# Two blocks and a mixture of experts on one core: the split operands of the mixers and of the third part at other byte offsets

## The chip, the core and the metric

The kernel runs on 1 core of one Trainium2 chip. The metric is the time of one execution in device microseconds, the median of the runs; lower is better. A profiled execution gives the trace from which the rows below are taken. Its span, from the first to the last instruction, is shorter than the execution's time, since start and end lie outside it.

## The reference

Two layers of a hybrid block, then a third block with a mixture of experts, all float32, on a sequence of 256 tokens with D = 1024:

```python
for i in range(2):
    x = x + 0.5 * swiglu(rms_norm(x, ffn1_norm[i]), ffn1_w_gate[i], ffn1_w_up[i], ffn1_w_down[i])
    h = rms_norm(x, mix_norm[i])
    proj = h @ w_in[i]
    z, xbc, dt_raw, q, k, v = jnp.split(proj, splits, axis=-1)
    y_ssd = ssd_mixer(silu(conv(xbc)), dt_raw, z, ...)
    y_att = dilated_attention(rms_norm(q), rms_norm(k), v)
    x = x + concatenate([y_ssd, y_att]) @ w_out[i]
    x = x + 0.5 * swiglu(rms_norm(x, ffn2_norm[i]), ...)
# third part: one more layer
u = modulate(rmsnorm(h, g_norm1), sh1, sc1)
proj = u @ w_in_2                       # conv branch, q, k, v, r, gates
h = h + ga1 * (gate0 * y_conv + gate1 * y_gla) @ w_out_2
u2 = modulate(rmsnorm(h, g_norm2), sh2, sc2)
h = h + ga2 * hierarchical_moe(u2, ...) # 32 experts
out = modulate(rmsnorm(h, g_final), shf, scf)
```

## The kernel before

Nearly every large product is split for accuracy: an operand A is held as a high part Ah, rounded to the float32r format, and a low part Al = A - Ah, and the product is three matmuls into one PSUM bank, high times low, low times high, high times high. The helper `three` (L776 to L782) issues them. Its arguments are `wh, wl` (the stationary operand, loaded into the array before each matmul) and `mh, ml` (the moving operand, streamed past it). In the rows of the profile a matmul reads `out<-moving,stationary`; so `misc<-xh,ring_low` streams xh past weights of ring_low, and `misc<-ring_low,xh` the other way round. The lines L780, L781 and L782 are those three matmuls, in that order.

The stages, in order of time:

- FFN 0, mixer 0, FFN 1, FFN 2, mixer 1, FFN 3 (two layers), then the third part with its own input projection, and the experts from about 1530 us on.
- An FFN (`ffn`, `gate_up`, `down`) streams the normalised rows xh, xl past the columns of the gate and up weights: high parts in `high_b`, low parts in `ring_low`. Each `gate_up` is 48 matmuls of 128x256. Then `down` streams weights (`high_r`, `ring_d_low`) past the hidden rows `hidh`, `hidl`, 12 matmuls of 128x512.
- A mixer first has 8 blocks of columns for the convolution; two of them unsplit, six split (`X_SPLIT`, in `ssd_and_projections`): xh, xl are the moving operand there, weights the stationary one. Then come 16 blocks through `project`, 48 matmuls each, in which the roles are swapped: weights (high parts in `ring_d_low` or `ue`, low parts in `ring_low`) move past xh, xl, 128 tokens at a time. Between the blocks stand short transposes and state products of the state-space scan. The out-projection later keeps its own split rows in the same space as xh, xl.
- The third part's input projection uses u2h (which lies on the space named `ue`) and u2l. `cols_split` has them as the moving operand, 21 blocks; `toks_split` has them as the stationary one, 4 blocks; 48 matmuls of 128x256 each. Between them stand the pair products (L1236) of the gated linear attention, whose data VectorE prepares.
- In the experts `ue` holds the gathered tokens as the stationary operand, weights move past in 512 columns.

SP's queue loads 1 MB blocks into a ring of 4 slots; a slot is freed by the last matmul that reads it. ACT rounds the high part, VectorE subtracts (`ring_low<-ring,...`). All of this is a fixed order written by hand; each engine runs its own stream and waits on semaphores.

**Where the operands lie.** All these buffers stand in one region of SBUF that begins with the ring. Bytes from the ring's start, modulo 512, follow from the sizes in the code. The rings take 12288 words, a multiple of 512 bytes. All parts have multiples of 128 words, except `xraw`, which has NX * (CONV_K - 1) = 48 words more (192 bytes). So whatever lies behind xraw is at 192, the rest at 0:

| operand | place before | place after |
|---|---|---|
| ring_low, ring_d_low, high_b, high_r, in_pc, in_rT | 0 | 0 |
| `ue` as weights of the mixers and tokens of the experts | 0 | 0 |
| xh, xl in the FFNs and in the out-projection | 192 | 192 |
| hidh, hidl | 192 | 192 |
| xh, xl in both mixers | 192 | 320 |
| u2h, u2l in the third part | 0 | 192 |

High and low halves of one operand lie a multiple of 512 bytes apart, and so do the slices of 128 or 256 words that one matmul takes.

Of the kernel before, what the change touches and what calls it, by code (L numbers as in the profile page):

```python
# [14 lines left out]
P = 128  # L15
SEQ = 256
# [24 lines left out]

# [93 lines left out]
def two_blocks(nc, d, out):  # L135
# [33 lines left out]
    with ctx:  # L169
# [11 lines left out]
        A_V2, A_PC, A_RT, A_OSQ = 6144, 8192, 10240, 26368  # L181
        rings = SLOTS * SLOT + SLOTS * SLOT_D
        A_Z = 2 * 2 * SEQ + NT * D + NX * (SEQ + CONV_K - 1) + NX * SEQ
# [23 lines left out]
        A_HIGH = 2 * 2 * SEQ + NT * D  # L207
# [3 lines left out]
        ue = over("ue", [KD, 2, 2 * CAP])  # L211
# [47 lines left out]
        xsc = part([NT, D])  # L259
        yatt = xsc  # L260
# [21 lines left out]
        yT = part([2 * KD, SEQ])  # L282
        btok = part([GROUPS, P])
# [20 lines left out]
        at[0] = 2 * 2 * SEQ + NT * D  # L304
# [22 lines left out]
        osq = part([KD, SEQ])  # L327
        zpad = part([NC2, SEQ + CONV_W - 1])
# [7 lines left out]
        u2h = ue[:, :, :, :].rearrange("p a b c -> p a (b c)")  # L336
# [16 lines left out]
        at[0] = here + 4 * GH * SEQ + 2 * GH * P + GH * P + KD * SEQ  # L353
# [3 lines left out]
        at[0] = A_X + 2 * KD * SEQ  # L357
# [24 lines left out]
        he = [a[:, :, :].rearrange("p a b -> p (a b)").rearrange("p (a b) -> p a b", a=CPE)  # L382
# [236 lines left out]
        def high_w(b):  # L619

            if b % HIGH_W < 2:
                return ring_d_low[:, 2 * (b % HIGH_W):2 * (b % HIGH_W) + 2, :].rearrange("p a b -> p (a b)")
            return ue[:, :, :, :].rearrange("p a b c -> p (a b c)")
# [153 lines left out]
        def _(pe):  # L777
# [57 lines left out]
            def first_gate_up(m0, n0, u):  # L835

                b = claim_bank(m0)
# [31 lines left out]
            def gate_up(m0, n0, i, c):  # L869
# [12 lines left out]
            def down(m0, n0, d0, g0, i, c, start, stop, between=()):  # L882
# [23 lines left out]
            def ffn(f, a, u, pieces=()):  # L906
# [5 lines left out]
                gate_up(m0, n0, 0, 1)  # L912
                pe.wait_ge(row_ready, u + 1)
                down(m0, n0, d0, NF * f, 0, 0, True, False)

                with pe.Fori(0, (NF - 2) // 4) as i:
                    for j in range(4):
                        gate_up(m0, n0, i, j + 2)
                        down(m0, n0, d0, NF * f, i, j + 1, False, False)
                for p in pieces[:1]:  # L920
                    modulation(p)
                down(m0, n0, d0, NF * f, 0, NF - 1, False, True, pieces[1:])
# [55 lines left out]
            def project(l, m, b):  # L978

                n = RING["win", l] + 8 + b  # L980
# [9 lines left out]
            def ssd_and_projections(l, a):  # L990
                n0 = RING["win", l]
                for j in range(8 - X_SPLIT):
# [698 lines left out]
        def _(act):  # L1691
# [29 lines left out]
            def rows_high(u, gain):  # L1721

                for q in range(4):
# [1589 lines left out]
```

## Time and profile before

| | |
|---|---|
| median of 3 runs | 2104.0 us |
| lowest, highest | 2101.42, 2104.66 us |
| span of the profiled execution | 2093.1 us |
| PE (matmul) busy | 2053.3 us, 98% |
| VectorE busy | 1644.7 us, 79% |
| ACT busy | 1212.5 us, 58% |
| DMA queues together | 61% of 16 engines' span, 230 GB/s |
| granted TensorE clock, mean | 0.997 |

The profiled execution's own time was not recorded apart from its span; the median of the runs is 10.9 us over the span. The page's busy time of PE counts the whole life of a matmul (some 276 ns for 256 columns), and these lives overlap, since the next matmul starts before the last has ended. What a matmul costs is the distance from its start to the start of the next, called its slot below. It is read from the view in order of time.

### The profile page before, as it was taken

The page shows a single profiled execution, that of the slowest core. Times are in us where ns is not written, and L with a number is a line of the kernel's source. Part 1 is how long each engine was busy: PE and PEld are TensorE (multiplying, and loading weights), DVE is VectorE, ACT ScalarE, POOL GpSimd, SP SyncE. Part 2 cuts the span into 40 slices and gives each one's busy share as a digit, 9 for nine tenths or more (in the row PEclk, how much of TensorE's full clock was granted, in tenths as well). Part 3 has the DMA queues.
Part 4 walks back from the last instruction along what each step waited for, and adds up shares of the span by engine and source line. Part 5 has one row for each costly group of instructions (what it writes and reads, how often), then busy time and mean ns, then how long its engine had stood idle before and what let it go on. Part 6 is the DMA issues. An engine that isn't in the chain of part 4 may idle for free. (4 is left out here: it accounts for less than half of the span.)

```text
span 2093.1 us, 35595 instructions
## 1 busy us (share of the span) xinstructions
PE 2053.3 (98%) x13737; PEld 1840.0 (88%) x13737; DVE 1644.7 (79%) x2070; ACT 1212.5 (58%) x1527; POOL 454.9 (22%) x237
## 2 busy tenths in 40 slices
PE   9999999999999999999999999999999999999997
PEld 8998999789999999999789998999877877777775
DVE  5776868557767875768557766998699999999998
ACT  5434565654435334565554335444378888888885
POOL 4982000007931990000008920000000000000000
PEclk9999999999999999999999999999999999999999
DMA  8875544247865775554257754445669999999994
GB/s 259 275 260 171 174 151 157 84 160 243 264 217 183 265 246 169 162 161 143 82 171 243 259 178 127 139 133 168 253 237 372 372 371 370 374 364 375 368 365 181
DMA packets 238937, 483.67 MB, mean 231 GB/s; under 512 B 10612, under 2 KB 178976, under 8 KB 222464
## 3 DMA queue, kind: packets, MB, share of 16 engines
q1 hardware_dynamic: 226880, 443.58, 60.5%
q0 software_dynamic: 11360, 37.21, 5.3%
q10 hardware_dynamic: 608, 1.65, 0.2%
q8 instruction: 61, 1.00, 0.2%
q14 instruction: 28, 0.23, 0.0%
HBM read 481.31 MB, written 1.09 MB: 230 GB/s over the span
## 5 line engine op out<-in xcount | busy, mean ns | idle before, releaser
L781 PE MATMUL misc<-xh,ring_low 128*128 128x256 f32 x1536 | 425.4, 277 | 0.0
L780 PE MATMUL misc<-xl,high_b 128*128 128x256 f32 x1344 | 372.6, 277 | 0.0
L782 PE MATMUL misc<-xh,high_b 128*128 128x256 f32 x1344 | 371.7, 277 | 0.0
L781 PEld LDWEIGHTS misc<-xh,ring_low 128*128 128x128 f32 x1536 | 289.0, 188 | 3.4
L3054 DVE TENSOR_TENSOR ring_low<-ring,high_b 128x2048 fp32r<-128x2048 f32 x128 | 287.0, 2283 | 0.6 <-issue 0.6
L1784 ACT ACTIVATE arena<-arena 128x256 f32<-128x256 f32 x88 | 36.8, 418 | 418.1 <-DVE arena L2391 418.1
L2354 DVE TENSOR_TENSOR ring_low<-ring,high_b 128x2048 fp32r<-128x2048 f32 x88 | 255.0, 2933 | 9.9 <-ACT high_b L1753 9.2
L780 PEld LDWEIGHTS misc<-xl,high_b 128*128 128x128 f32 x1344 | 252.3, 188 | 3.4
L2104 ACT ACTIVATE high_b<-ring 128x2048 fp32r<-128x2048 f32 x124 | 235.8, 1914 | 32.6 <-DMA ring<-in_w_dram 31.9
L782 PEld LDWEIGHTS misc<-xh,high_b 128*128 128x128 f32 x1344 | 252.4, 188 | 0.0
L1666 POOL TENSOR_SCALAR arena<-arena,cact 128x1024 f32<-128x1024 f32 x56 | 214.4, 3829 | 6.8 <-DMA arena<-in_w_ada_dram 3.5
L1430 PE MATMUL misc<-high_b,ue 128*128 128x512 f32 x512 | 203.4, 397 | 2.8 <-DVE ue L3097 1.2
L1432 PE MATMUL misc<-ring_low,ue 128*128 128x512 f32 x512 | 199.9, 390 | 0.0
L1663 POOL TENSOR_SCALAR arena<-arena,cact 128x1024 f32<-128x1024 f32 x4 | 14.4, 3604 | 714.3 <-DVE hidl L2376 706.7
L1753 ACT ACTIVATE high_b<-ring 128x2048 fp32r<-128x2048 f32 x88 | 163.4, 1903 | 4.8 <-DMA ring<-in_ffn_w_up_dram 2.9
L3060 DVE TENSOR_TENSOR ring_d_low<-ring_d,high_r 128x1024 fp32r<-128x1024 f32 x128 | 147.8, 1213 | 0.5
L780 PE MATMUL misc<-ring_low,xh 128*128 128x256 f32 x512 | 146.1, 285 | 1.3 <-DVE arena L2543 1.3
L2391 DVE TENSOR_TENSOR arena<-misc,row_rstd 128x256 f32<-128x256 f32 x88 | 37.0, 420 | 137.8 <-PE misc L782 127.0
L2109 ACT ACTIVATE high_r<-ring_d 128x1024 fp32r<-128x1024 f32 x128 | 131.5, 1054 | 13.5 <-DMA ring_d<-in_w_dram 12.5
L782 PE MATMUL acc<-high_r,hidh 128*128 128x512 f32 x352 | 138.6, 394 | 0.0
L781 PE MATMUL acc<-high_r,hidl 128*128 128x512 f32 x352 | 138.1, 392 | 0.0
L780 PE MATMUL acc<-ring_d_low,hidh 128*128 128x512 f32 x352 | 137.2, 390 | 0.0
(483 smaller groups left out, 5169.3 us busy)
## 6 DMA issues: line engine op xcount, KB each, us to landing
ring<-in_w_dram SPq DMA_DIRECT2D x128, 1024.0 KB, 7.9
ring<-in_w_in_dram SPq DMA_DIRECT2D x72, 1024.0 KB, 5.4
ring_d<-in_w_dram SPq DMA_DIRECT2D x128, 512.0 KB, 5.3
ring<-in_ffn_w_gate_dram SPq DMA_DIRECT2D x44, 1024.0 KB, 5.5
ring<-in_ffn_w_up_dram SPq DMA_DIRECT2D x44, 1024.0 KB, 8.4
ring_d<-in_ffn_w_down_dram SPq DMA_DIRECT2D x88, 512.0 KB, 7.5
arena<-in_w_ada_dram POOLq DMA_DIRECT2D x48, 512.0 KB, 5.1
ring<-in_w_out_dram SPq DMA_DIRECT2D x20, 1024.0 KB, 5.0
```

Source lines behind the costliest of these rows:

```text
L780: pe.matmul(dst, wh, ml, start=start, stop=False, **kw)
L781: pe.matmul(dst, wl, mh, start=False, stop=False, **kw)
L782: return pe.matmul(dst, wh, mh, start=False, stop=stop, **kw)
L1430: pe.matmul(b, ue[:, k, half, :], expert_part(high_b, x)[:, kk, :], start=(k == 0), stop=False)
L1432: mm = pe.matmul(b, ue[:, k, half, :], expert_part(ring_low, x)[:, kk, :], start=False, stop=(k == KD - 1))
L1666: pool.tensor_scalar(row, row, cact[:, k:k + 1], None, ALU.mult).then_inc(pool_step, 1)
L1753: act.activation(high_b[:, s, :], ring[:, s, :], ACT.Copy).then_inc(high_in[s], 1)
L2104: act.activation(high_b[:, s, :], ring[:, s, :], ACT.Copy).then_inc(high_in[s], 1)
L2109: act.activation(high_r[:, s, :], ring_d[:, s, :], ACT.Copy).then_inc(high_in_d[s], 1)
L2354: dve.tensor_tensor(ring_low[:, s, :], ring[:, s, :], high_b[:, s, :].bitcast(F32), ALU.subtract)\
L3054: dve.tensor_tensor(ring_low[:, s, :], ring[:, s, :], high_b[:, s, :].bitcast(F32), ALU.subtract)\
L3060: dve.tensor_tensor(ring_d_low[:, s, :], ring_d[:, s, :], high_r[:, s, :].bitcast(F32), ALU.subtract).then_inc(low_in_d[s], 1)
```

## The change

The spaces of u2h, of hidh and hidl, and of xh and xl each become one flat tensor, 128 words (512 bytes) longer than needed, and the arena's parts get pads of the same size. Views of these tensors are taken at a first word that depends on the use: 32 words (128 bytes) in the two mixers (uses 1 and 4), 48 words (192 bytes) for u2h and u2l, 0 elsewhere. No instruction is added, removed or moved; each engine has the same stream with other addresses.

```diff
+LINES = 128
+SHIFT_X = {0: 0, 1: 32, 2: 0, 3: 0, 4: 32, 5: 0}
+SHIFT_HID = {0: 0, 1: 0, 2: 0, 3: 0}
+SHIFT_U2 = 48
...
-        A_V2, A_PC, A_RT, A_OSQ = 6144, 8192, 10240, 26368
+        A_V2, A_PC, A_RT, A_OSQ = (LINES + a for a in (6144, 8192, 10240, 26368))
...
-                nc.sbuf_tensor("pad_osq", [P, A_OSQ - A_RT - KD * SEQ], F32), \
+                nc.sbuf_tensor("pad_osq", [P, A_OSQ - A_RT - KD * SEQ + SHIFT_U2], F32), \
                 nc.sbuf_tensor("u2l", [P, KD, SEQ], F32R) as u2l:
...
-        A_HIGH = 2 * 2 * SEQ + NT * D
+        A_HIGH = 2 * 2 * SEQ + NT * D + LINES
...
-        ue = over("ue", [KD, 2, 2 * CAP])
+        u2_rows = over("u2_rows", [2 * KD * 2 * CAP + LINES])
+        ue = u2_rows[:, 0:2 * KD * 2 * CAP].rearrange("p (a b c) -> p a b c", a=KD, b=2)
...
-        hidh, hidl = over("hidh", [2, SEQ]), over("hidl", [2, SEQ])
+        hidhl = over("hidhl", [2 * 2 * SEQ + LINES])
         beside(A_X)
-        xh, xl = over("xh", [KD, SEQ]), over("xl", [KD, SEQ])
+        xhl = over("xhl", [2 * KD * SEQ + LINES])
+        rows_at = {u: halves_of(xhl, SHIFT_X[u], KD) for u in SHIFT_X}
+        xh, xl = halves_of(xhl, 0, KD)
...
-        u2h = ue[:, :, :, :].rearrange("p a b c -> p a (b c)")
+        u2h = u2_rows[:, SHIFT_U2:SHIFT_U2 + KD * SEQ].rearrange("p (a b) -> p a b", a=KD)
...
             def project(l, m, b):
+                xh, xl = rows_at[3 * l + 1]
...
-                act.activation(xh[:, :, :], xnT[:, :, :], ACT.Copy).then_inc(xs_high, 1)
+                act.activation(rows_at[3 * l + 1][0], xnT[:, :, :], ACT.Copy).then_inc(xs_high, 1)
```

## Rows read from the trace of the kernel before

**Rows 1.** The page, part 1: busy time of the two busiest engines.

```profile
PE 2053.3 (98%) x13737; PEld 1840.0 (88%) x13737; DVE 1644.7 (79%) x2070; ACT 1212.5 (58%) x1527; POOL 454.9 (22%) x237
```

**Rows 2.** Busy time by window, core 0, columns as in the first line.

```profile
core 0: us, PE busy (x) PEld busy (x) DVE busy (x) ACT busy (x) POOL busy (x), PEclk, DMA share, GB/s
215.00:252.00 37.00, 37.00 (x325) 36.90 (x324) 31.51 (x48) 20.05 (x21) 0.00 (x0) 1.00 0.56 171
252.00:362.00 110.00, 109.35 (x923) 108.70 (x922) 78.87 (x84) 66.79 (x109) 0.00 (x0) 1.00 0.50 154
1282.00:1484.00 202.00, 200.52 (x1549) 195.60 (x1549) 176.92 (x254) 96.75 (x87) 2.67 (x5) 1.00 0.50 165
```

**Rows 3.** Waits of PE in 215:363 and in 1280:1484: total, times, longest (us).

```profile
PE misc L780 <- DVE arena L2543: 0.7, 1, 0.7
...
PE misc L780 <- DVE ring_low L2707: 1.5, 2, 1.3
```

**Rows 4.** Split products by tile: count, duration min/median/max (ns), first and last start (us).

```profile
L780 PE MATMUL misc<-ring_low,xh x512: 279/280/469, 252.0 to 986.9; 128*128 128x256 f32 x171
...
L782 PE MATMUL misc<-xh,ring_d_low x128: 276/281/281, 216.1 to 867.9; 128*128 128x256 f32 x128
...
L782 PE MATMUL misc<-xh,ue x64: 276/278/283, 226.9 to 876.9; 128*128 128x256 f32 x64
...
L781 PE MATMUL misc<-ue,ring_low x336: 280/283/283, 1283.0 to 1483.6; 128*128 128x256 f32 x168
```

**Rows 5.** PE in order of time (start, life in us), FFN 0; last two rows 41 slots apart.

```profile
62.37 0.28 PE L780 MATMUL misc<-xl,high_b 128*128 128x256 f32 x1
62.49 0.28 PE L781 MATMUL misc<-xh,ring_low 128*128 128x256 f32 x1
...
62.72 0.28 PE L780 MATMUL misc<-xl,high_b 128*128 128x256 f32 x1
...
67.37 0.28 PE L782 MATMUL misc<-xh,high_b 128*128 128x256 f32 x1
```

**Rows 6.** The same view, split columns of mixer 0, 239 slots apart.

```profile
216.18 0.28 PE L780 MATMUL misc<-xl,ring_d_low 128*128 128x256 f32 x1
...
243.27 0.28 PE L782 MATMUL misc<-xh,ue 128*128 128x256 f32 x1
```

**Rows 7.** The same view, split columns of mixer 1, 214 slots apart.

```profile
843.06 0.28 PE L781 MATMUL misc<-xh,ring_low 128*128 128x256 f32 x1
...
868.26 0.28 PE L782 MATMUL misc<-xh,ue 128*128 128x256 f32 x1
```

**Rows 8.** The same view, a block of `project` in mixer 0, 41 slots apart.

```profile
272.45 0.28 PE L780 MATMUL misc<-ring_low,xh 128*128 128x256 f32 x1
...
277.28 0.28 PE L782 MATMUL misc<-ring_d_low,xh 128*128 128x256 f32 x1
```

**Rows 9.** Third part: `cols_split`, 181 slots apart, and `toks_split`, 39 slots apart.

```profile
1284.07 0.28 PE L781 MATMUL misc<-ue,ring_low 128*128 128x256 f32 x1
...
1305.79 0.28 PE L782 MATMUL misc<-ue,ring_d_low 128*128 128x256 f32 x1
...
1331.03 0.28 PE L780 MATMUL misc<-ring_low,ue 128*128 128x256 f32 x1
...
1335.71 0.28 PE L780 MATMUL misc<-ring_low,ue 128*128 128x256 f32 x1
```

**Rows 10.** First blocks of FFN 1 (44 slots apart) and of FFN 2 (44 slots apart).

```profile
457.03 0.28 PE L781 MATMUL misc<-xh,ring_low 128*128 128x256 f32 x1
...
462.21 0.28 PE L780 MATMUL misc<-xl,high_b 128*128 128x256 f32 x1
...
645.94 0.28 PE L780 MATMUL misc<-xl,high_b 128*128 128x256 f32 x1
...
650.93 0.28 PE L782 MATMUL misc<-xh,high_b 128*128 128x256 f32 x1
```

**Rows 11.** A window in the third part where VectorE is busiest (columns as in Rows 2).

```profile
1352.00:1362.00 10.00, 8.72 (x75) 8.53 (x74) 9.93 (x19) 1.52 (x3) 0.00 (x0) 1.00 0.33 106
```

More of the change, by code:

```diff
@@ L216, in two_blocks, with halves_of @@
         beside(A_HID)
-        hidh, hidl = over("hidh", [2, SEQ]), over("hidl", [2, SEQ])
+        def halves_of(a, first, k):
+            n = k * SEQ
+            return [a[:, first + i * n:first + (i + 1) * n].rearrange("p (k s) -> p k s", k=k) for i in range(2)]
+        hidhl = over("hidhl", [2 * 2 * SEQ + LINES])
         beside(A_X)
-        xh, xl = over("xh", [KD, SEQ]), over("xl", [KD, SEQ])
+        xhl = over("xhl", [2 * KD * SEQ + LINES])
+        hid_at = {f: halves_of(hidhl, SHIFT_HID[f], 2) for f in SHIFT_HID}
+        hidh, hidl = halves_of(hidhl, 0, 2)
+        rows_at = {u: halves_of(xhl, SHIFT_X[u], KD) for u in SHIFT_X}
+        xh, xl = halves_of(xhl, 0, KD)
         beside(ARENA)
@@ L259, in two_blocks @@
         xsc = part([NT, D])
+        part([LINES])
         yatt = xsc
@@ L282, in two_blocks @@
         yT = part([2 * KD, SEQ])
+        part([LINES])
         btok = part([GROUPS, P])
@@ L327, in two_blocks @@
         osq = part([KD, SEQ])
+        part([LINES])
         zpad = part([NC2, SEQ + CONV_W - 1])
@@ L835, in first_gate_up @@
             def first_gate_up(m0, n0, u):
+                xh, xl = rows_at[u]
                 b = claim_bank(m0)
@@ L867, in first_gate_up, with gate_up @@
                 mm.then_inc(filled, 1)
-            def gate_up(m0, n0, i, c):
+            def gate_up(m0, n0, u, i, c):
+                xh, xl = rows_at[u]
                 b = claim_bank(m0, i, c)
@@ L880, in gate_up, with down @@
                 mm.then_inc(filled, 1)
-            def down(m0, n0, d0, g0, i, c, start, stop, between=()):
+            def down(m0, n0, d0, f, i, c, start, stop, between=()):
+                g0 = NF * f
+                hidh, hidl = hid_at[f]
                 pe.wait_ge(hid_low, i * 4 + (g0 + c + 1))
@@ L911, in ffn @@
                 row_of_rstd(u)
-                gate_up(m0, n0, 0, 1)
+                gate_up(m0, n0, u, 0, 1)
                 pe.wait_ge(row_ready, u + 1)
-                down(m0, n0, d0, NF * f, 0, 0, True, False)
+                down(m0, n0, d0, f, 0, 0, True, False)
                 with pe.Fori(0, (NF - 2) // 4) as i:
                     for j in range(4):
-                        gate_up(m0, n0, i, j + 2)
-                        down(m0, n0, d0, NF * f, i, j + 1, False, False)
+                        gate_up(m0, n0, u, i, j + 2)
+                        down(m0, n0, d0, f, i, j + 1, False, False)
                 for p in pieces[:1]:
                     modulation(p)
-                down(m0, n0, d0, NF * f, 0, NF - 1, False, True, pieces[1:])
+                down(m0, n0, d0, f, 0, NF - 1, False, True, pieces[1:])
             def cols_out(m0, n0, i, j, src=xnT, u=None):
@@ L991, in ssd_and_projections @@
                 n0 = RING["win", l]
+                xh, xl = rows_at[3 * l + 1]
                 for j in range(8 - X_SPLIT):
@@ L1721, in rows_high @@
             def rows_high(u, gain):
+                xh = rows_at[u][0]
                 for q in range(4):
@@ L2333, in rows_low @@
             def rows_low(u, gain):
+                xh, xl = rows_at[u]
                 m0 = FILL["norm", u]
@@ L2361, in low_rows, with hidden @@
                     .then_inc(low_in_d[s], 1)
-            def hidden(g0, m0, d0, i, c):
+            def hidden(f, m0, d0, i, c):
+                g0 = NF * f
+                hidh, hidl = hid_at[f]
                 dve.wait_ge(gate_ready, i * 4 + (g0 + c + 1))
```

19 lines of the change are left out of this document (10 added, 9 removed).

## The prediction

> **What bounds the kernel.** I read the page first, for the busy shares: PE is busy 98% of the span, VectorE 79% [rows 1]. The view by windows then gives the two stages that the change touches: PE is busy 37.0 of 37 us in the split columns of the first mixer, 109.35 of 110 us in its `project` blocks and 200.52 of 202 us in the third part's input projection [rows 2]. The view of waits says how little PE waits for others there: 0.7 us in a mixer, 1.5 us in the third part [rows 3]. The granted clock is 1.00 in all of these windows [rows 2], the upper level of 2.4 GHz. So in these stages time is matmuls times slot, where a slot is the distance between two starts, and a slot that gets shorter shortens the kernel, unless another engine is nearly as late.
>
> The change adds and removes nothing. What it can change is the slot of the split products whose operands move. The view of PE in order of time has slots of one shape (128x256, float32r, three per product) in three sizes. With "distance" for the place of the moving operand minus the place of the stationary one, modulo 512 bytes (places from the table above):
>
> - distance 192, FFN: 4.65 us over 41 slots, 113.4 ns [rows 5]. 80 of the FFNs' blocks, all that follow a `down`, look like this after their first five slots.
> - distance 192, split columns of mixer 0: 27.09 us over 239 slots, 113.3 ns [rows 6].
> - distance 192, the same columns of mixer 1, same code and same addresses: 25.20 us over 214 slots, 117.8 ns [rows 7].
> - distance 320 (which is -192), `project`: 4.83 us over 41 slots, 117.8 ns [rows 8]. All 32 blocks of both mixers look like this.
> - distance 0, third part, in both roles: 21.72 us over 181 slots and 4.68 us over 39 slots, 120.0 ns [rows 9].
>
> Two things follow. First, place matters: nothing else separates the third part from the FFNs, and swapping the roles within the third part changes nothing. Secondly, at distance 192 there are two rhythms, and a block keeps the one that it falls into at its start: the first block of FFN 1 stays at 117.7 ns (5.18 us over 44), the first of FFN 2 runs at 113.4 (4.99 us over 44) [rows 10]. After a `down` it was always the fast one. After other work it was fast in 2 of 6 stretches, which hold 284 of 664 slots, or 43%. The loading of the next weights and the streaming of the present operand run side by side and read the same memory; I take it that they hinder each other at certain distances, and that the start fixes their phase.
>
> **The change part by part.** After it, `project` is at distance 0 - 320 = 192, the third part's `cols_split` at 192, the mixers' split columns at 320 and `toks_split` at -192 = 320. All FFN and expert operands keep their distance modulo 512, though some (high_b against ring_low) move by 512. The two 128-column halves of a weight block already differ by 512 and show one slot [rows 5], so I cost that at nothing.
>
> 1. `project`: 3 x 512 = 1536 matmuls [rows 4], now 117.8. Bounds at distance 192: 113.3 (saves 6.9 us) and 117.8 (saves nothing). These blocks start after short matmuls, as the 43% above do, so I take half of the blocks fast: 1536 x 2.25 ns = 3.4 us saved.
> 2. `cols_split`: 3 x 336 = 1008 matmuls [rows 4], now 120.0. Bounds 113.3 (6.7 us) and 117.8 (2.2 us). With half the blocks fast: 1008 x 4.45 ns = 4.5 us saved.
> 3. `toks_split`: 4 blocks of 48, 192 matmuls, 120.0 to 117.8: 0.4 us saved.
> 4. The mixers' split columns: 3 x (128 + 64) = 576 matmuls [rows 4], half in each mixer. At distance 320 the only rhythm seen is 117.8 [rows 8]. Mixer 1 is there already; mixer 0 pays 288 x 4.5 ns = 1.3 us. Bounds: 0 (the fast rhythm survives) and 576 slots at 120, 1.9 + 0.6 = 2.5 us.
> 5. What does not pass through. In the third part VectorE is busy 9.93 of 10 us around 1352 us and PE 8.72 [rows 11]: PE waits for the level products there, so what `toks_split` saves (0.4 us), and some 0.2 us behind it, only lengthens that wait. The window as a whole leaves VectorE 202 - 176.9 = 25 us of idle time against at most 7 us of savings [rows 2], so the rest passes. In each mixer PE already waits once for VectorE before a transpose [rows 3], and two blocks lie under such chains: 2 x 2 x 48 x 2.25 ns = 0.4 us. Together 1.0 us.
> 6. ACT and VectorE write the moved rows with the same instructions; experts and DMA start earlier by what is saved. Zero for both, since the rings are freed by PE's own matmuls.
>
> Sum: -3.4 - 4.5 - 0.4 + 1.3 + 1.0 = -6.0 us, on the profiled span 2093.1 to 2087.1. The median is 10.9 us over the span, and that part is untouched: 2104.0 - 6.0 = **2098.0 us**. Ends of this case: all blocks fast, -6.9 - 6.7 - 0.4 + 1.3 + 1.5 = -11.2, or 2092.8; no block of `project` fast and only a part of the third part's, -3, or 2101.
>
> **The rivals.**
>
> *No new block finds the fast rhythm.* For it: 32 of 32 `project` blocks run at 117.8 today, and three of four first blocks of an FFN stay slow at distance 192. Against it: at another distance the start differs too. Price: 0 - 2.2 - 0.4 + 1.3 + 0.2 = -1.1 us, 2102.9 us.
>
> *VectorE takes over the third part.* It is busy 176.9 of 202 us there [rows 2], with stretches at 99% [rows 11]. If its waits lie badly, steps 2 and 3 are lost and the mixers alone are left, -3.4 + 1.3 + 0.4 = -1.7 us, 2102.3 us. Against it: PE waits for it 1.5 us in all in that stage [rows 3].
>
> *Addresses do not matter.* Slots of 113.3, 117.8 and 120.0 ns would come from what stands around the blocks, and the time would stay at 2104.0 us. For it: rows 6 and rows 7 differ at equal addresses. Against it: the third part has 120.0 ns in every block, with both roles, and the FFNs never. The Trainium skill speaks for this rival: "TensorE: Matmul & The Clock Gate" (section "Step-by-step: what each phase is for") has two independent read ports, so that loading the next weights takes nothing from the running matmul, and "SBUF — State Buffer" (section "Who interferes with whom") says that PE never waits on anyone. By that page's columns over clock a slot of 256 columns would be, by an estimate, about 109 ns everywhere. The trace disagrees: no stretch of these products is under 113.3 ns, and the surplus differs by stage.
>
> *The new place 320 is worse than any seen* (the slower side). Single slots of 122 ns stand in the first five slots of many blocks of the FFNs (from 62.37 to 62.49 us, at the resolution of the view) [rows 5]. If the pair 0 against 320 kept such a slot, in either role, `project` would lose 1536 x 4.2 = 6.5 us, the split columns 288 x 8.7 + 288 x 4.2 = 3.7 us, and against the third part's -4.9 + 0.6 the sum is +5.9 us, 2109.9 us. It decides from an average of about 119.2 ns (117.2 now, and 4.3 us over 2112 matmuls) over the mixers' 2112 matmuls upwards, where it eats what the third part gives. Against it: modulo 512 the new distances, 192 and 320, are both old ones, and neither lasts at 122 in any block.
>
> **How the numbers follow.** Forecast (half of the blocks or more fast): 0.62. No new fast block: 0.16. VectorE takes over: 0.06. Addresses without effect: 0.05. The new place is worse: 0.07. The rest, 0.04, is for something not seen, to either side. A difference of 0.2% is 4.2 us, about what a measurement of this kernel can tell from none; faster by that means under 2099.8 us. Of the forecast's 0.62 some 0.56 lie there, since its upper end does not, and half of the rest and chance add a little: faster 0.6. Slower (over 2108.2 us) is the last rival and a little more: 0.08. The rest, 0.32, is within 0.2%. The range goes from all blocks fast less the scatter of medians, 1.8 us (the lowest run is 2.6 us below the median), 2091 us, up to the case with no fast block, 2103 us. It leaves out the two last rivals and the rest, 0.16.
>
> **What would show it.** Right: in the view of PE in order of time, `misc<-ring_low,xhl` blocks with 113.3 ns slots and some with 117.8; third part blocks at 113.3 or 117.8, none at 120.0; mixer 0's split columns at 117.8; FFN blocks unchanged at 113.3 after `down`. The third part's window shortens by 4 to 5 us, `project`'s 110 us by some 2 us in each mixer. Wrong: 120 ns or more in `project` (the place is bad), 120.0 ns still in the third part (addresses do not matter), new waits of PE for VectorE above 2 us in the third part (VectorE took over), or FFN slots that changed, in which case a distance counts over more than 512 bytes.

## The result, and the profile after the change

| | before | after |
|---|---|---|
| median | 2104.0 us (5 runs, 2098.56 to 2104.66) | 2091.47 us (5 runs, 2090.13 to 2093.20) |
| time of the profiled execution | not recorded | 2090.46 us |
| its span | 2093.1 us | 2088.7 us |
| its mean granted clock | 0.997 | 0.997 |

The ratio of after to before is 0.9949, with an interval of 0.9936 to 0.9963: faster, by 12.5 us of the medians. The two spans differ by 4.4 us only. Which of the two is the effect is the question of the experiments; a comparison over more runs (e8_again, below) says 0.998, with an interval of 0.9967 to 0.9992, which is 4.2 us.

The kernel after has other line numbers and tile names: the three matmuls of a split product are L797, L798 and L799, xh and xl are both `xhl`, and `ue` and u2h are `u_rows`. The page, part 1, answers to [rows 1]:

```profile
PE 2048.2 (98%) x13737; PEld 1833.4 (88%) x13737; DVE 1647.5 (79%) x2070; ACT 1211.7 (58%) x1527; POOL 456.0 (22%) x237
```

The same matmuls (x13737), the same shares. The windows of the three stages, set by the starts of the stages in this trace, answer to [rows 2] (busy us and count of PE, PEld, DVE, ACT, POOL, then granted clock, DMA share, GB/s):

```profile
215.00:253.00 38.00, 38.00 (x319) 37.74 (x319) 31.52 (x48) 20.72 (x21) 0.00 (x0) 1.00 0.55 167
253.00:363.00 110.00, 109.35 (x935) 108.70 (x934) 79.01 (x86) 66.76 (x109) 0.00 (x0) 1.00 0.49 154
1283.00:1481.00 198.00, 196.22 (x1552) 191.19 (x1551) 175.18 (x254) 96.42 (x87) 2.67 (x5) 1.00 0.52 168
```

In 110 us of `project` PE now starts 935 matmuls where it started 923. The third part's projection does in 198 us what took 202 us (1552 and 1549 matmuls). The split columns need 1 us more. PE in order of time (start, life) shows the slots behind it. A block of `project` in mixer 0 that is fast now, 41 slots from the first to the last row, against [rows 8]; then the last block of the same mixer, again 41 slots:

```profile
301.98 0.28 PE L797 MATMUL misc<-ring_low,xhl 128*128 128x256 f32 x1
...
306.63 0.28 PE L799 MATMUL misc<-ring_d_low,xhl 128*128 128x256 f32 x1
...
342.31 0.28 PE L797 MATMUL misc<-ring_low,xhl 128*128 128x256 f32 x1
...
347.14 0.28 PE L799 MATMUL misc<-ring_d_low,xhl 128*128 128x256 f32 x1
```

4.65 us over 41 is 113.4 ns; 4.83 us over 41 is 117.8 ns, the old slot. In mixer 0 the 7 blocks from 294.4 to 335.2 us are fast, in mixer 1 the 8 from 912.0 to 958.6 us; all others stay at 117.8. The third part, against [rows 9]: a stretch of `cols_split` over 185 slots, one over 41 slots, and a block of `toks_split` over 41 slots:

```profile
1284.31 0.28 PE L797 MATMUL misc<-u2l,ring_d_low 128*128 128x256 f32 x1
...
1305.27 0.28 PE L799 MATMUL misc<-u_rows,ring_d_low 128*128 128x256 f32 x1
...
1307.88 0.28 PE L797 MATMUL misc<-u2l,ring_d_low 128*128 128x256 f32 x1
...
1312.71 0.28 PE L799 MATMUL misc<-u_rows,ring_d_low 128*128 128x256 f32 x1
...
1330.01 0.28 PE L797 MATMUL misc<-ring_low,u_rows 128*128 128x256 f32 x1
...
1334.84 0.28 PE L799 MATMUL misc<-ring_d_low,u_rows 128*128 128x256 f32 x1
```

20.96 us over 185 is 113.3 ns; the other two are 117.8 ns. No block is at 120.0 any more. The split columns of mixer 0, 200 slots apart, against [rows 6], are at 23.56 / 200 = 117.8 ns:

```profile
217.44 0.28 PE L798 MATMUL misc<-xhl,ring_low 128*128 128x256 f32 x1
...
241.00 0.28 PE L797 MATMUL misc<-xhl,ring_d_low 128*128 128x256 f32 x1
```

And the FFNs are as they were [rows 5]; the second block of FFN 0, 41 slots, 113.4 ns:

```profile
29.33 0.28 PE L797 MATMUL misc<-xhl,high_b 128*128 128x256 f32 x1
...
33.98 0.28 PE L799 MATMUL misc<-xhl,high_b 128*128 128x256 f32 x1
```

The waits of PE for VectorE, here over the whole trace (waiter, releaser, total, times, longest), stay small. The third part's goes from 1.5 to 1.8 us; the mixers' is 0.7 us once in each, as it was [rows 3]:

```profile
PE misc L797 <- DVE ring_low L2740: 1.8, 2, 1.4
...
PE misc L797 <- DVE arena L2576: 1.3, 2, 0.7
```

**The balance of the two traces.** I cut both spans at the first and last product of each kind. Times in us; mean slots over all split products of the stage that follow one another.

| stage | before | after | | mean slot before, after (ns) |
|---|---|---|---|---|
| FFN 0 | 182.8 | 181.6 | -1.2 | 114.06, 114.03 |
| from FFN 0 to the split columns | 19.7 | 21.4 | +1.7 | |
| split columns, mixer 0 | 36.6 | 37.7 | +1.1 | 113.41, 117.56 |
| `project`, mixer 0 | 109.7 | 108.3 | -1.4 | 117.78, 115.98 |
| split columns, mixer 1 | 37.8 | 37.6 | -0.2 | 117.85, 117.52 |
| `project`, mixer 1 | 109.7 | 108.1 | -1.6 | 117.78, 115.71 |
| from FFN 3 to the third part's split products | 23.7 | 25.3 | +1.6 | |
| third part, split products | 200.7 | 196.0 | -4.7 | cols 119.90, 115.32; toks 119.83, 117.80 |
| all others | 1372.4 | 1372.7 | +0.3 | FFNs 1 to 3 at 114.0 to 114.1 in both |

The stages with moved operands give -1.4 - 1.6 - 4.7 + 1.1 - 0.2 = -6.8 us. The two +1.7 and +1.6 have nothing to do with addresses. In each lies a stretch in which the granted clock drops to 0.50, the lower level of 1.2 GHz. Windows of after, around 201 and 1269 us:

```profile
199.00:201.00 2.00, 1.83 (x16) 1.86 (x16) 0.56 (x2) 2.00 (x6) 0.00 (x0) 0.96 0.06 18
201.00:204.00 3.00, 3.00 (x8) 2.46 (x9) 0.43 (x3) 2.97 (x5) 0.00 (x0) 0.50 0.00 0
...
1269.00:1273.00 4.00, 4.00 (x14) 1.62 (x14) 1.43 (x4) 0.00 (x0) 1.16 (x2) 0.57 0.05 11
```

and of before, around the same work:

```profile
201.00:204.00 3.00, 3.00 (x18) 2.72 (x18) 0.43 (x3) 2.97 (x6) 0.00 (x0) 1.00 0.00 0
...
1269.00:1273.00 4.00, 4.00 (x25) 2.43 (x25) 1.43 (x4) 0.02 (x1) 1.16 (x2) 1.00 0.06 15
```

In 3 us PE starts 8 matmuls instead of 18. Each such stretch lasts 3.4 us. The first comes behind 16 matmuls of one column (128x1, from 199.2 us, after an idle time of 0.5 us), the second behind 16 of 36 columns (from 1267.5 us, after one of 1.4 us). Before had one too, at 13.0 us, behind 2.4 us in which PE stood idle at the start of FFN 0 (about the 1.2 us of the first line of the table). Which places have one differs from execution to execution of all kernels here. So by the traces the change is worth 6 to 7 us, of which this one pair of executions shows 4.4.

### The profile page after: what moved, and what is told of

Its sections match the earlier page's. It is cut to its first block and busy times, and to the rows that moved or that the text cites. A ratio compares the mean times of both kernels' runs of the same rounds, so it can differ in the third digit from the quotient of the medians.

```text
span 2088.7 us, 35595 instructions
## 1 busy us (share of the span) xinstructions
PE 2048.2 (98%) x13737; PEld 1833.4 (88%) x13737; DVE 1647.5 (79%) x2070; ACT 1211.7 (58%) x1527; POOL 456.0 (22%) x237
## 5 line engine op out<-in xcount | busy, mean ns | idle before, releaser
L798 PE MATMUL misc<-xhl,ring_low 128*128 128x256 f32 x1536 | 425.4, 277 | 0.0
L797 PE MATMUL misc<-xhl,high_b 128*128 128x256 f32 x1344 | 372.6, 277 | 0.0
L799 PE MATMUL misc<-xhl,high_b 128*128 128x256 f32 x1344 | 371.6, 277 | 0.0
L798 PEld LDWEIGHTS misc<-xhl,ring_low 128*128 128x128 f32 x1536 | 288.9, 188 | 3.4
L797 PEld LDWEIGHTS misc<-xhl,high_b 128*128 128x128 f32 x1344 | 252.3, 188 | 3.4
L799 PEld LDWEIGHTS misc<-xhl,high_b 128*128 128x128 f32 x1344 | 252.4, 188 | 0.0
L1456 PE MATMUL misc<-high_b,u_rows 128*128 128x512 f32 x512 | 203.3, 397 | 2.8 <-DVE u_rows L3130 1.2
L1458 PE MATMUL misc<-ring_low,u_rows 128*128 128x512 f32 x512 | 199.9, 391 | 0.0
L797 PE MATMUL misc<-ring_low,xhl 128*128 128x256 f32 x512 | 145.7, 285 | 1.3 <-DVE arena L2576 1.3
L799 PE MATMUL acc<-high_r,hidhl 128*128 128x512 f32 x352 | 138.6, 394 | 0.0
L798 PE MATMUL acc<-high_r,hidhl 128*128 128x512 f32 x352 | 138.0, 392 | 0.0
L797 PE MATMUL acc<-ring_d_low,hidhl 128*128 128x512 f32 x352 | 137.2, 390 | 0.0
```

The source lines that it names most:

```text
L797: pe.matmul(dst, wh, ml, start=start, stop=False, **kw)
L798: pe.matmul(dst, wl, mh, start=False, stop=False, **kw)
L799: return pe.matmul(dst, wh, mh, start=False, stop=stop, **kw)
L1456: pe.matmul(b, ue[:, k, half, :], expert_part(high_b, x)[:, kk, :], start=(k == 0), stop=False)
L1458: mm = pe.matmul(b, ue[:, k, half, :], expert_part(ring_low, x)[:, kk, :], start=False, stop=(k == KD - 1))
```

## The experiments

Theory A: the slot of a split product depends on the distance between the places of its two operands; the modulus is 512 bytes or less; at 192 there are two rhythms, 113.3 and 117.8 ns; at 64 or 320, 117.8; at 0, 120.0. The time saved is the sum of the slots. Rival B: the new arrangement of memory as such (the pads) does it, not the distance of a pair. Rival C: most of the 12.5 us is scatter of medians.

Shifts below are in words of 4 bytes; use 0 is FFN 0, 1 and 4 are the mixers, 2 and 3 are FFNs 1 and 2, 5 is FFN 3. All are edits of the kernel after.

### The arrangement without the shifts

```diff
-SHIFT_X = {0: 0, 1: 32, 2: 0, 3: 0, 4: 32, 5: 0}
+SHIFT_X = {0: 0, 1: 0, 2: 0, 3: 0, 4: 0, 5: 0}
-SHIFT_U2 = 48
+SHIFT_U2 = 0
```

> All shifts 0: only the flat spaces and the pads of 512 bytes stay. Theory (the distance modulo 512 bytes between the moving and the stationary operand sets the slot, with two rhythms at distance 192): project blocks 117.8 ns, third part 120.0 ns, third part's projection window about 200.7 us, time equal to the kernel before within its scatter. Rival (the pads and the 512-byte move of the upper buffers bring the gain): the time of the changed kernel, some 12 us under before, with the third part still at 120.0 ns or not. Rival (the medians differ for another reason than the slots, such as stretches at half clock): this kernel could be anywhere between, with slots as before.

Measured: 2098.84 us (12 runs, 2095.0 to 2105.03) against 2097.82 (29 runs, 2092.84 to 2113.84), ratio 1.0008 [0.9994, 1.0021]. `project` is at 117.78 ns in both mixers, the third part at 119.91 and 119.87: as before, to 0.1 ns. B falls. This also says what the median of before is: 29 runs give 2097.82, not 2104.0, so C has its first support. Scatter alone may not be all of it: of the first five runs of before three took 2104.0 us or more, but only four of the 68 runs of before beside e1_layout, e8_again and e9_out that took about 2100 us. Those three comparisons ran on chips 7, 12 and 10; the chip of the first is not on record. What made its before so long stays open.

A surprise stands in FFN 0, whose operands have the distance of before. All of its blocks run at 117.8 ns, also those behind a `down`. The split columns of mixer 1 have changed the other way, to 113.4 ns where before had 117.85 at the same places. 41 slots of a block of this run, 4.83 us:

```profile
62.42 0.28 PE L797 MATMUL misc<-xhl,high_b 128*128 128x256 f32 x1
...
67.25 0.28 PE L799 MATMUL misc<-xhl,high_b 128*128 128x256 f32 x1
```

FFN 0 took 185.9 us for it, where the trace after has 181.6. The other FFNs of the same run are at 114.05 ns.

### The mixers alone, and the third part alone

```diff
 SHIFT_X = {0: 0, 1: 32, 2: 0, 3: 0, 4: 32, 5: 0}
-SHIFT_U2 = 48
+SHIFT_U2 = 0
```

> Only the mixers' xh, xl at 320, third part as before. Theory: per mixer the project stage falls from 109.7 to about 108.2 us, mixer 0's split columns cost up to 1.1 us more, third part 200.7 us: sum about -2 us against all shifts 0. Rival (project gains nothing by itself): +1 us. Rival (the whole 12.5 us are the mixers'): -12 us.

```diff
-SHIFT_X = {0: 0, 1: 32, 2: 0, 3: 0, 4: 32, 5: 0}
+SHIFT_X = {0: 0, 1: 0, 2: 0, 3: 0, 4: 0, 5: 0}
 SHIFT_U2 = 48
```

> Only u2h, u2l at 192, mixers as before. Theory: the third part's projection window falls from 200.7 to about 196 us, mixers' project stage 109.7 us each: sum about -4.7 us against all shifts 0. Rival (VectorE holds the third part): under -1 us. Rival (additive with something unseen): -10 us.

Mixers alone: 2095.26 us (12 runs, 2090.61 to 2100.78), ratio 0.9985 [0.9967, 1.0004]. Its `project` blocks are at 115.20 ns in mixer 0 and 116.73 in mixer 1 (107.9 and 109.1 us instead of 109.7), its third part at 119.90 and 119.89. The split columns of mixer 0, at distance 320, stay at 113.33: the fast rhythm exists there too. Third part alone: 2095.39 us (12 runs, 2090.41 to 2101.18), ratio 0.9987 [0.9974, 1.0001]. Its mean slots are those of after, 115.32 and 117.77, in 196.0 us instead of 200.7; `project` is at 117.78. So each half of the change shortens the slots of its own stage alone. By the ratios they are worth 3.1 us (between 6.9 less and 0.8 more) and 2.7 us (5.4 less and 0.2 more), 5.8 us together; each alone is at the edge of what the comparison can tell from nothing.

This trace also shows a rhythm being lost inside FFN 0. Two blocks that follow one another, 41 slots each: 4.64 us (113.2 ns), then 4.83 us (117.8 ns):

```profile
79.81 0.28 PE L797 MATMUL misc<-xhl,high_b 128*128 128x256 f32 x1
...
84.45 0.28 PE L799 MATMUL misc<-xhl,high_b 128*128 128x256 f32 x1
...
88.05 0.28 PE L797 MATMUL misc<-xhl,high_b 128*128 128x256 f32 x1
...
92.88 0.28 PE L799 MATMUL misc<-xhl,high_b 128*128 128x256 f32 x1
```

From there on every block up to FFN 0's end is slow; its mean is 116.42 ns.

### Other distances

```diff
-SHIFT_X = {0: 0, 1: 32, 2: 0, 3: 0, 4: 32, 5: 0}
+SHIFT_X = {0: 16, 1: 64, 2: 32, 3: 96, 4: 96, 5: 64}
-SHIFT_U2 = 48
+SHIFT_U2 = 96
```

> Places of xh, xl by use: FFN 0 256, mixer 0 448, FFN 1 320, FFN 2 64, mixer 1 64, FFN 3 448; u2h, u2l at 384. So distances (moving minus stationary, modulo 512): FFNs 256, 320, 64, 448; project 64 and 448; split columns 448 and 64; third part 384 in the columns, 128 in the tokens. Theory: the slot depends on the distance alone, whichever operand moves: FFN 2, mixer 0's project and mixer 1's split columns agree (64), FFN 3, mixer 1's project and mixer 0's split columns agree (448), FFN 1 shows 117.8 ns and not 113.3 after a down (320). Rival (the place of one operand alone counts): project and columns with the same place agree instead of those with the same distance. Rival (addresses do not matter): all FFNs 113.3 after a down.

One run: 2106.99 us, span 2105.2. Slots by distance: FFN 0 at 256, 119.90 ns; FFN 1 at 320, 117.80; FFN 2 at 64, 117.63; FFN 3 at 448, 114.06; `project` at 64 (mixer 0), 117.78, and at 448 (mixer 1), 115.98; the third part at 384, 118.66, and at 128, 119.03. Two of its blocks, 41 slots each, FFN 0 at 256 and mixer 1's `project` at 448:

```profile
54.29 0.28 PE L797 MATMUL misc<-xhl,high_b 128*128 128x256 f32 x1
...
59.21 0.28 PE L799 MATMUL misc<-xhl,high_b 128*128 128x256 f32 x1
...
945.95 0.28 PE L797 MATMUL misc<-ring_low,xhl 128*128 128x256 f32 x1
...
950.60 0.28 PE L799 MATMUL misc<-u_rows,xhl 128*128 128x256 f32 x1
```

4.92 us is 120.0 ns, and 4.65 us is 113.4. Distance 256 is as 0, 320 as 64, 448 as 192: **the period is 256 bytes**, not the 512 of the prediction. And at 64 and at 192 the same slots (117.8, and 113.3 beside it at 192) stand in FFNs, in the split columns and in `project`, whichever operand moves; the means differ, since they mix the two rhythms. At 128 only the third part has rows, 118.66 ns in its columns and 119.03 in its tokens.

### Distances off the 64-byte grid

```diff
-SHIFT_X = {0: 0, 1: 32, 2: 0, 3: 0, 4: 32, 5: 0}
+SHIFT_X = {0: 4, 1: 28, 2: 8, 3: 60, 4: 36, 5: 56}
-SHIFT_U2 = 48
+SHIFT_U2 = 52
```

> Distances modulo 256 in steps of 16 bytes: FFN 0 208, FFN 1 224, FFN 2 176, FFN 3 160; project 208 in mixer 0 and 176 in mixer 1 (their split columns 48 and 80); third part columns 208, tokens 48. Theory (period 256 bytes, and a fast rhythm of 113.3 ns that exists only around 192): slots near 113.3 within 16 bytes of 192, 117.8 to 120 farther off, and the same distance gives the same slots in FFN, project and third part. A width of the good region of 32 bytes or more would show all of 176, 192, 208 alike. Rival (only steps of 64 bytes count, such as a line of memory): 208 and 224 look like 192 or like 256 (120.0), without values between. Rival (a better distance exists): a slot under 113.3, down to the 109 ns of the transposes.

```diff
-SHIFT_X = {0: 0, 1: 32, 2: 0, 3: 0, 4: 32, 5: 0}
+SHIFT_X = {0: 12, 1: 24, 2: 52, 3: 62, 4: 40, 5: 2}
-SHIFT_U2 = 48
+SHIFT_U2 = 44
```

> The other distances: FFN 0 240, FFN 1 144, FFN 2 184, FFN 3 200; project 224 and 160 (split columns 32 and 96); third part columns 176, tokens 80. Theory: FFN 2 and FFN 3 (8 bytes off 192) stay at 113.3 after a down; FFN 0 (240) tends to 120.0 as 256 did; FFN 1 (144) lies between the 119 ns of 128 and the rest. Rival (a better distance exists beside 192): one of them under 113.3 or without the slow rhythm in any block.

One run each: 2118.14 and 2117.88 us, spans 2116.3 and 2116.1. Mean slots by distance modulo 256, all stages of both:

| distance | slot (ns) | where |
|---|---|---|
| 32, 48 | 116.70, 118.32 | split columns |
| 48 | 117.78 | third part, tokens |
| 80, 96 | 119.71, 119.97 | split columns |
| 80 | 118.01 | third part, tokens |
| 144 | 117.59 | FFN 1 |
| 160 | 118.73, 118.20 | FFN 3, `project` |
| 176 | 119.27, 118.82, 118.22 | FFN 2, `project`, third part's columns |
| 184, 200 | 119.97, 120.14 | FFNs 2, 3 |
| 208 | 119.10, 118.78, 117.84 | FFN 0, `project`, third part's columns |
| 224 | 118.31, 118.27 | FFN 1, `project` |
| 240 | 117.20 | FFN 0 |

Sixteen bytes beside 192 the slot is 117.8 to 119.3 ns, and eight bytes beside it 120.0 and 120.1. No mean is below 113.3. In a block of FFN 0 at 208, 41 slots take 4.89 us, 119.3 ns:

```profile
54.42 0.28 PE L797 MATMUL misc<-xhl,high_b 128*128 128x256 f32 x1
...
59.31 0.28 PE L799 MATMUL misc<-xhl,high_b 128*128 128x256 f32 x1
```

So of the distances tried 192 is the one where the fast rhythm is common, and it has to be met closely. The expectations had a good region around 192, 113.3 ns still at 8 bytes beside it, and 120.0 near 240; all three are wrong (240 has 117.20). And off the grid of 64 bytes the distance alone does not give the slot: at 80 it is 119.71 in one stage and 118.01 in another, at 176 and 208 the stages differ by over 1 ns. Split columns of mixer 1 in e5_fine_a and a block of the tokens in e6_fine_b, both at distance 80, take 5.04 us (120.0 ns) and 4.97 us (118.3 ns) for 42 slots:

```profile
859.02 0.28 PE L799 MATMUL misc<-xhl,ring_d_low 128*128 128x256 f32 x1
...
864.06 0.28 PE L799 MATMUL misc<-xhl,ring_d_low 128*128 128x256 f32 x1
```

```profile
1354.67 0.28 PE L799 MATMUL misc<-ring_d_low,u_rows 128*128 128x256 f32 x1
...
1359.64 0.28 PE L799 MATMUL misc<-ring_d_low,u_rows 128*128 128x256 f32 x1
```

What else counts there is open.

### The kernel after again, and the hidden rows moved

The first is the kernel after, unchanged, for a comparison over more runs. The second has, beside the change, other places for hidh and hidl, the stationary operand of `down`:

```diff
-SHIFT_HID = {0: 0, 1: 0, 2: 0, 3: 0}
+SHIFT_HID = {0: 32, 1: 32, 2: 48, 3: 16}
```

> The changed kernel once more, to set its time against many more runs of the kernel before, and for a second trace. Theory (a block falls into one of two rhythms at distance 192, by nanoseconds at its start): the same blocks of project can come out otherwise than in the first trace, the third part's window is again near 196 us, and the time is 5 to 7 us (0.3%) under the kernel before, not 12.5. Rival (the 12.5 us of the first comparison are real): 0.6% again.

> On top of the change, hidh and hidl in the FFNs at places 320 (FFN 0 and 1), 384 (FFN 2) and 256 (FFN 3), so that the down products go from distance 64 (modulo 256) to 192, 128 and 0. Theory (192 is the best distance): their slots, 226 to 232 ns by line before, fall in FFN 0 and 1 and rise in FFN 3; 264 matmuls per FFN, so 4 ns would be 1.1 us each. The gate_up blocks that follow may fall into the other rhythm (117.8 instead of 113.3, 3.9 us per FFN), since down sets how they start. Rival (a 512-column matmul hides the load of the next weights at any distance): down slots unchanged in all four FFNs.

Again: 2095.19 us (12 runs, 2087.73 to 2100.49) against 2099.39 (23 runs, 2093.32 to 2106.29), ratio 0.998 [0.9967, 0.9992]. The slots are those of the first trace of after (`project` 115.71 and 115.72, third part 115.32 and 117.77). So the change is faster, and its size is 4.2 us, between 1.7 and 6.9, in which both the 6.0 us of the forecast and the 6.8 us of the stage balance lie; the 12.5 us of the first medians do not. The 8.3 us between them did not come back, which is C, with the open question above on what they were. The scatter of one kernel, 13 us from 2087.73 to 2100.49, is larger than the effect.

Hidden rows moved: 2101.54 us (10 runs, 2099.84 to 2109.42), ratio 1.0014 [1.0001, 1.0028], slower than the kernel after by some 6 us. Its FFNs take 11.5 us more than in the first trace of after, and the larger part, 9.0 us by its slots, is in neighbours. `gate_up`, whose operands did not move, goes from 114.05 to 115.75, 115.91 and 115.67 ns in FFNs 0 to 2, and to 117.61 in FFN 3. A block of FFN 3, 41 slots in 4.83 us:

```profile
1156.86 0.28 PE L797 MATMUL misc<-xhl,high_b 128*128 128x256 f32 x1
...
1161.69 0.28 PE L799 MATMUL misc<-xhl,high_b 128*128 128x256 f32 x1
```

`down` itself (512 columns) starts its three products 227.6, 229.4 and 231.7 ns apart in FFN 3 of the kernel after (distance 64), and 227.8, 226.8 and 226.7 in FFN 3 of this run (distance 0), but 232 to 234 in FFNs 0 and 1 (distance 192). Not all of that need be the distance: in FFN 0 of e1_layout, with `down`'s operands at their old places beside slow blocks, the mean of the three is 230.5 ns, and it is 229.0 in the kernel after. So the place of `down`'s operand takes part in setting the rhythm of the next `gate_up`: with it unmoved, FFNs 1 to 3 had 114.0 to 114.1 ns at distance 192 in every trace. FFN 3 is the clearest: a `down` that is 2.5 ns a product quicker comes with 3.5 ns more in each of the 1029 slots of `gate_up`.

### The out-projection's rows at distance 0

Both operands of the third part's out-projection are at distance 0 and start 226 to 227 ns apart; the mixers' (yh at 192) start 230 to 233 ns apart. This run moves the high part of the mixers' rows y by 64 bytes:

```diff
-        xh, xl = halves_of(xhl, 0, KD)
+        yh = halves_of(xhl, SHIFT_Y, KD)    # SHIFT_Y = 16
...
         def y_high_of(k):
-            return (xh if k < KD else xl)[:, k % KD, :]
+            return yh[k // KD][:, k % KD, :]
```

> The changed kernel, and beside it the rows y of the mixers' out-projection move by 64 bytes (16 words), so that their distance to the 512-column operand streamed past them is 0 in place of -192 (equal to 64 modulo 256). In the trace of the changed kernel the 512-column products of this stage start 232.9 ns (ring_low with xhl), 230.6 ns (high_b) and 232.7 ns (ring_d_low with xhl) apart, 96 of each in both mixers; in the third part, where all operands are at distance 0, the same products start 226 to 227 ns apart. Theory (for 512 columns distance 0 is the best, as run e7_hidden's down products suggested, in reverse to 256 columns): all three kinds come to 227, which is 96 x (5.9 + 3.6 + 5.7) = 1.46 us less in the span, -0.7 us in each mixer's out-projection, and a ratio to the kernel before of about 0.997, a shade under that of the changed kernel alone. Rival (the 512-column slots are set by something else, such as the split writes of the other engines during the mixer): the slots stay at 230 to 233 ns and the time is that of the changed kernel. Project, split columns and third part keep their slots in either case (115.7, 117.5, 115.3).

Measured: 2094.73 us (12 runs, 2086.12 to 2100.25), ratio 0.9975 [0.9961, 0.9989] against 2098.6, the median of 16 runs of before (two more took 4158.69 and 6382.34 us and are left out). But the stage is 88.3 us in both mixers where it was 88.4. The three products of mixer 0 start 234.4, 228.6 and 232.8 ns apart (out_low with y high, out_high with y low, out_high with y high), for 232.9, 230.5 and 232.7 in the kernel after: a mean of 231.9 for 232.0. The theory for 512 columns falls: the sum is as before, with a little moved from the second to the first. The shift also did less than the expectation says. y's low part lies in `high_b`, so the second product kept its operands in place, and yet it is the one that got faster; and a third of the weights' high parts lie in `in_z`, which is at 192 like all that lies behind xraw, so that their product with y high went from distance 0 to 192 (233.2 to 234.9 ns) while that of the others went from 64 to 0 (232.7 to 232.0). What makes 227 in the third part is open. The ratio is that of the kernel after within its interval.

The profiled execution, 2099.43 us, shows one thing that scatters. Windows around 201 and 1508 us of this run, and 1505 to 1516 us of the kernel after, which has the same work:

```profile
201.00:208.00 7.00, 7.00 (x23) 5.83 (x23) 3.49 (x5) 6.97 (x8) 0.00 (x0) 0.52 0.01 2
1508.00:1519.00 11.00, 11.00 (x58) 11.00 (x57) 7.26 (x30) 6.75 (x9) 0.09 (x1) 0.53 0.49 198
```

```profile
1505.00:1516.00 11.00, 11.00 (x101) 10.91 (x100) 7.98 (x33) 6.75 (x9) 1.07 (x2) 1.00 0.57 232
```

The lower clock stays for 6.8 us at 201.3 us and for 10.2 us at 1508.6 us, two and three times the 3.4 us seen elsewhere, and the stages around them take 23.0 and 50.9 us instead of 19.7 and 46.1: 1.6 us for each 3.4 us.

### High and low rows at different distances

```diff
-        rows_at = {u: halves_of(xhl, SHIFT_X[u], KD) for u in SHIFT_X}
+        rows_at = {u: (halves_of(xhl, SHIFT_X[u], KD)[0], halves_of(xhl, SHIFT_L[u], KD)[1]) for u in SHIFT_X}
...
-SHIFT_X = {0: 0, 1: 32, 2: 0, 3: 0, 4: 32, 5: 0}
+SHIFT_X = {0: 0, 1: 32, 2: 32, 3: 0, 4: 32, 5: 32}
+SHIFT_L = {0: 32, 1: 32, 2: 64, 3: 32, 4: 32, 5: 64}
```

> The changed kernel, and in the FFNs the high rows xh and the low rows xl stand at different distances to the weights: xh 192 and xl 64 in FFNs 0 and 2, xh 64 and xl 192 in FFNs 1 and 3 (all modulo 256). Two of three products of a gate_up stream xh, one streams xl. Theory A (each product has the slot of its own distance): 114.8 ns a slot in FFNs 0 and 2 = (2 x 113.3 + 117.8)/3, and 116.3 in FFNs 1 and 3, the three lines of a triple showing different gaps; by 3072 such products in each FFN, FFNs 0 and 2 longer by some 2 us each and 1 and 3 by some 7 us each against the changed kernel. Theory B (a block as a whole falls into one of two rhythms, and the fast one needs all of its operands at 192): 117.8 in every block of all four FFNs, about +11 us each. Theory C (the fast rhythm is held once the high rows are at 192): FFNs 0 and 2 unchanged at 114, FFNs 1 and 3 at 117.8.

One run: 2112.61 us, span 2110.8. The four FFNs have mean slots of 117.78, 117.66, 117.76 and 117.68 ns, with 0 to 2% of their slots at the fast 113 to 114 ns where the kernel after has 85%. That is theory B of this run: the fast rhythm needs all three products at 192. (My "+11 us each" there, and the sizes of A, counted too many products; an FFN has 1029 such slots, which makes 3.8 us, and FFN 0 measures 187.7 us, 4.9 over the 182.8 of the repetition, FFNs 1 and 2 together 381.5, 9.5 over, FFN 3 188.0, 4.4 over. The 1.1 us of FFN 0 beyond the 3.8 are in `down`, whose operands stayed: 233.3 ns for 229.2.) The three lines of a triple differ, which A wanted, but not as it wanted. In FFNs 0 and 2 the gap behind the product that streams xl (distance 64) is 119.7 ns and the gaps behind the two that stream xh (192) are 117.4 and 116.2; in FFNs 1 and 3 it is 116.7 behind xl (192), 118.3 and 118.0 behind xh (64). A product at distance 192 does not reach 113.3 while a neighbour is at 64. Three triples in order of time, in which each start is 0.11 or 0.12 us behind the last, and a triple takes 0.36 or 0.35 us:

```profile
56.98 0.28 PE L798 MATMUL misc<-xhl,high_b 128*128 128x256 f32 x1
57.10 0.28 PE L799 MATMUL misc<-xhl,ring_low 128*128 128x256 f32 x1
57.22 0.28 PE L800 MATMUL misc<-xhl,high_b 128*128 128x256 f32 x1
57.34 0.28 PE L798 MATMUL misc<-xhl,high_b 128*128 128x256 f32 x1
57.45 0.28 PE L799 MATMUL misc<-xhl,ring_low 128*128 128x256 f32 x1
57.57 0.28 PE L800 MATMUL misc<-xhl,high_b 128*128 128x256 f32 x1
57.69 0.28 PE L798 MATMUL misc<-xhl,high_b 128*128 128x256 f32 x1
```

## Why the prediction was right, and where it was not

The forecast was 2098.0 us in a range of 2091 to 2103, faster most likely; the median was 2091.47, just inside, and faster. By its steps:

- **Step 1, `project`, -3.4 us with half of the blocks fast.** Right in mechanism, and in size in this execution. 15 of 32 blocks are fast (7 and 8). The stages are 1.4 + 1.6 = 3.0 us shorter, and the slots give the same: 768 x 1.80 + 768 x 2.07 ns = 3.0 us. The half was a guess, and the trace has 42 and 48% of the slots fast. In both traces of the kernel after the first blocks of a mixer are slow and a later run of them fast. But other runs differ: over the 13 stages of `project` at distance 192 in all traces here 90 of 208 blocks are fast, from 1 of 16 (mixer 0 of e10_apart, 0.2 us less than before) to 11 of 16 (mixer 1 of the same run, 1.9 us less), and the second and third block can be fast too. So half is about the mean, and that one execution met it is partly luck.
- **Steps 2 and 3, third part, -4.5 and -0.4 us.** Right. The mean of `cols_split` is 115.32 ns for the 115.55 of half and half (115.95 or 115.96 in three later runs), `toks_split` 117.80 for 117.8. The stage gave 4.7 us; with step 5's share of 0.6 I had 4.3.
- **Step 4, split columns, +1.3 us.** +1.1 in mixer 0, and -0.2 in mixer 1. The sentence that only one rhythm exists at 320 was wrong in a corner: in two runs (mixers alone, mixer 0, 113.33 ns; hidden rows moved, mixer 1, 113.33 ns) these columns ran fast at that distance. In the kernel after itself the last of the six blocks is fast where slots follow one another, in both mixers, which is the -0.2; and in e7_hidden one block of `toks_split`, from 1354.8 us, runs at 113.3 ns at distance 64.
- **Step 5, what does not pass, +1.0 us.** Too much by 0.7 us. In the third part the slots give 1008 x 4.58 ns + 192 x 2.03 ns = 5.0 us, of which 4.7 arrived; the missing 0.3 us is the growth of PE's wait for VectorE, 1.5 to 1.8 us. In the mixers all arrived, and the wait kept its 0.7 us.
- **Step 6, zero.** Right: FFNs 1 to 3 are at 114.0 to 114.1 ns in both traces, and the rest differs by 0.3 us.

The sum of -6.0 us stands against -6.8 in the stages that hold moved operands. **The step that failed is the base**: "The median is 10.9 us over the span, and that part is untouched: 2104.0 - 6.0". In every run here whose span and time are both known an execution takes 1.8 us (1.7 to 1.9) more than its span. So the profiled execution before, with a span of 2093.1 us, took some 2095 us, and the 2104.0 of three runs was 9 us above it: before's median was 2097.82 in 29 later runs and 2099.39 in 23. Why those three were so high stays open, as said under the arrangement without the shifts. Its span plus 1.8 less 6.0 would be 2088.9; from its wider medians, 2092 to 2093; the kernel after had 2091.47 in 5 runs and 2095.19 in 12. The first of these lies only 0.5 us inside a range whose lower end stood for all blocks fast; what brought it there was the base and not the slots, so that it lies inside is partly luck. I took a difference that I could not explain for a constant. The spread of 3.2 us over three runs, which the range used as scatter of medians (1.8 us), was too small: 12 runs of one kernel spread over 10 to 14 us.

What scatters is known in part. A stretch at granted clock 0.50 costs 1.6 us per 3.4 us, and the profiled executions have 1 to 6 of them before the last 12 us; FFN 0 in the slow rhythm costs 3.8 us of slots (e1_layout; all of 1029 slots by 3.7 ns). Of the seven profiled executions with FFN 0's operands and hidden rows at their old places one had it wholly slow and one lost the fast rhythm midway. The clock stretches are not shown to account for the rest.

Two premises were wrong without harm to the sum. "Distance modulo 512": the period is 256, shown by e4_sweep; the shift of 128 bytes makes 320, equal to 64, and its counterpart is 192 in `project` by either modulus. And "a block keeps the rhythm that it falls into at its start, after a `down` always the fast one": e3_third loses the fast one behind a `down` at 87 us, e1_layout never has it in FFN 0, and e7_hidden loses it in FFN 3 by moving `down`'s operand.

The rivals. *No new fast block* is refuted by 15 fast blocks. *VectorE takes over* is refuted by its wait, 0.3 us longer. *Addresses do not matter* is refuted by the arrangement without shifts beside the others, and by e4_sweep: one operand moved by 64 bytes in FFN 0 made 119.90 ns of 114.03. So the slot is not the same everywhere, as this rival took from the Trainium skill, and its estimate of 109 ns was met by no stretch of these products; that figure is the Trainium skill's on "TensorE: Matmul & The Clock Gate" (section "Step-by-step: what each phase is for"), not of the page on SBUF. Whether the two read ports disturb each other no run shows. That the loading of the next weights and the streaming disturb each other when they fall on the same piece of memory would fit what stands on the grid of 64 bytes, but no run shows the collision itself; the last run, in which a product pays for its neighbour's distance, speaks for something between successive matmuls. *The new place is worse* did not happen: nothing lasts at 122.

## What to carry to other kernels

Where PE is the bound and its products are short (256 columns of float32r), look at the slots in order of time and sort the stages by the byte distance between the two operands modulo 256; here a shift of one operand by 64 to 192 bytes was worth up to 6 ns in 120, and the best distance, 192, has to be met closely (8 bytes beside it cost as much as distance 0), by all products of a sequence. Judge such a change by the slots and the durations of the stages it touches, not by medians of a few runs that scatter by more than the effect. Where only one rhythm occurs they repeat to 0.1 ns and 0.2 us; where there are two, take several executions, since one stage of `project` gained between 0.2 and 1.9 us. And never carry the difference between a median and one span as a constant: ask first what an execution costs over its own span.

## What the runs showed of the hardware

- The slot of a split product of 256 columns depends on the distance of moving and stationary operand with a period of 256 bytes: 113.3 or 117.8 ns at 192, mostly 117.8 at 64, 118.7 to 119.0 at 128, 120.0 at 0, and 116.7 to 120.1 between the multiples of 64. At 0, 64 and 192 the levels are the same whichever of the two operands moves; between the multiples of 64 they are not (80: 119.71 in the split columns, 118.01 in the third part's tokens).
- At 192, and seldom at 64, there are two stable rhythms, at equal code and equal addresses. Which one a stretch has is set by the work ahead of it, and it can differ between executions (FFN 0: 114.03, 116.42 and 117.71 ns).
- Products of 512 columns (`down`, out-projection) have slots of 226 to 236 ns. Their three lines share the time differently when an operand moves, and the mean moves by 5 ns at most; distance 0 was the best once (FFN 3 of e7_hidden, 227) and no help the other time (e9_out, 231.9 for 232.0). They also change with the rhythm of the blocks beside them (229.2 to 233.3 ns in FFN 0 of e10_apart, own operands unmoved). The rule is open.
- The granted clock falls to 0.50 for 3.4 us, or two or three times that, behind idle time or very small matmuls (128x1, 128x36) of PE, at places that change between executions.
- No rearrangement that was tried gave more than the change itself.
